# Second model: every projection of a layer's middle in one block, with the state space, step sizes, convolutions, rotation and compression woven in

## The reference, cut to what matters

```
h = rmsnorm(x, attn_norm_w[l])
proj = h @ w_in[l]        # 512 x 1024 by 1024 x 2964
(z, xbc, dt_raw, sc_b, sc_c, sc_h, q, k_c, v_c, k_s, v_s, k_w, v_w, g_nsa) = split(proj)
xbc = silu(causal_dwconv(xbc, conv_w, conv_b))         # 4 taps; gives x, B and C
dt  = softplus(dt_raw + dt_bias)                       # 8 heads
y   = state space: (decay * (C B^T)) (x dt) + x d_skip, then * silu(z), then rmsnorm over 512
y_sc = sc_b * causal_dwconv(sc_c * sc_h, sc_conv_w)    # 3 taps
q, k_c, k_s, k_w are rotated; k_c and v_c are cut into 31 overlapping blocks of 32 tokens,
kc = gelu(blocks(k_c) @ w1) @ w2, vc likewise; gates = sigmoid(g_nsa)
y_nsa = sparse attention over kc/vc, k_s/v_s, k_w/v_w
x = x + concat[y, y_sc, y_nsa] @ w_out;   then a convolved feed-forward
```

## Time and profile before

| | us |
|---|---|
| median of 2 runs (4588.11 to 4590.89) | 4589.5 |
| the profiled execution's own time | 4589.26 |
| its span, first to last instruction | 4587.5 |
| middle of layer 0, first projection matmul to first attention matmul | 282.03 |
| middle of layer 1, the same | 281.80 |

### The profile page before, as it was taken

One profiled execution on the slowest core, in us unless ns is written; L12 is line 12 of the kernel. 1 busy time (PEld: TensorE's weight loads), 2 busy tenths in 40 slices (PEclk: granted clock), 3 DMA queues, 4 the chain that ended last, 5 costly groups with the idle time before them and its releaser, 6 DMA issues. The chain is left out here.

```text
span 4587.5 us, 53132 instructions
## 1 busy us (share of the span) xinstructions
PE 4016.8 (88%) x19582; PEld 3037.8 (66%) x19582; DVE 2268.3 (49%) x3774; ACT 1573.5 (34%) x2671; POOL 299.2 (7%) x292
## 2 busy tenths in 40 slices
PE   4896988998999898878899899886879988678998
PEld 2553566777788795645666688664568877456886
DVE  7777674223653562355532555243455524454552
ACT  2044534112442442245421343233344423333431
POOL 1201010001000000000000100102010010201001
PEclk8997999999999999989999999997899999788999
DMA  6602020111222352000022233220123322012332
GB/s 234 202 8 69 18 96 29 56 61 53 92 96 99 115 165 85 35 17 10 24 69 87 81 98 99 81 75 19 38 64 97 100 98 79 14 33 73 96 98 81
DMA packets 83413, 348.84 MB, mean 76 GB/s; under 512 B 9152, under 2 KB 9536, under 8 KB 79680
## 3 DMA queue, kind: packets, MB, share of 16 engines
q1 hardware_dynamic: 69440, 296.59, 20.0%
q0 software_dynamic: 13824, 50.34, 3.4%
HBM read 344.80 MB, written 2.10 MB: 76 GB/s over the span
## 5 line engine op out<-in xcount | busy, mean ns | idle before, releaser
L556 DVE TENSOR_TENSOR split_low<-weight_ring,split_high 128x1024 fp32r<-128x1024 f32 (+1 forms) x412 | 534.3, 1297 | 818.5 <-ACT split_high L548 818.2
L548 ACT ACTIVATE split_high<-weight_ring 128x1024 fp32r<-128x1024 f32 (+1 forms) x430 | 477.9, 1113 | 969.5 <-PE banks L1197 466.2
L1325 PE MATMUL banks<-normed_high,split_high 128*128 128x512 f32 (+1 forms) x1760 | 652.5, 371 | 79.1 <-DVE normed_low L440 37.9
L1325 PE MATMUL banks<-normed_low,split_high 128*128 128x512 f32 (+1 forms) x1760 | 650.1, 369 | 0.0
L1325 PE MATMUL banks<-normed_high,split_low 128*128 128x512 f32 (+1 forms) x1760 | 649.7, 369 | 0.0
L1325 PEld LDWEIGHTS banks<-normed_high,split_high 128*128 128x128 f32 x1760 | 333.9, 190 | 139.9 <-issue 84.4
L1325 PEld LDWEIGHTS banks<-normed_low,split_high 128*128 128x128 f32 x1760 | 334.1, 190 | 55.4
L1325 PEld LDWEIGHTS banks<-normed_high,split_low 128*128 128x128 f32 x1760 | 333.7, 190 | 55.1
L1197 PE MATMUL banks<-hidden_high,split_high 128*128 128x512 f32 (+1 forms) x880 | 325.0, 369 | 7.2 <-DVE split_low L556 7.2
L1197 PE MATMUL banks<-hidden_low,split_high 128*128 128x512 f32 (+1 forms) x880 | 324.5, 369 | 0.0
L1197 PE MATMUL banks<-hidden_high,split_low 128*128 128x512 f32 (+1 forms) x880 | 324.4, 369 | 0.0
(11 more groups left out here) (235 smaller groups left out, 6550.7 us busy)
## 6 DMA issues: line engine op xcount, KB each, us to landing
weight_ring<-in_up SPq DMA_DIRECT2D x220, 512.0 KB, 3.5
weight_ring<-in_down SPq DMA_DIRECT2D x80, 704.0 KB, 4.0
modulation_ring<-in_ada POOLq DMA_DIRECT2D x96, 512.0 KB, 4.5
weight_ring<-in_merge SPq DMA_DIRECT2D x48, 768.0 KB, 4.2
weight_ring<-in_out SPq DMA_DIRECT2D x32, 512.0 KB, 3.5
weight_ring<-in_diff SPq DMA_DIRECT2D x12, 1024.0 KB, 5.5
weight_ring<-in_xbc SPq DMA_DIRECT2D x16, 512.0 KB, 3.7
weight_ring<-in_window SPq DMA_DIRECT2D x6, 1024.0 KB, 4.8
```

The lines of the kernel that those rows point to most:

```text
L548: act.activation(k.splits[0][:, (n0 + panel) % RING, 0:width], k.slot(n0 + panel)[:, 0:width], ACT.Copy).then_inc(k.high_ready.sem, 1)
L556: dve.tensor_tensor(k.splits[1][:, s, 0:width], k.ring[:, s, 0:width], k.splits[0][:, s, 0:width].bitcast(F32), ALU.subtract).then_inc(k.l ...
L1325: last = pe.matmul(sums(r, half), w, x, start=(c + j == 0), stop=(c == KT - 1 and j == 2))
```

## The change

`project_split`, `short_convolution`, `step_sizes`, `state_space` and `compress` go, and with them the separate norm and rotation blocks. `second_branches` runs one block of 25 jobs, from the norm to the end of the compression. Job 0 is a new full panel that holds dt (columns 0 to 7) and the gates (32 to 43) feature-major, in place of the 20-column token-major jobs. Jobs 1 to 8 are the convolved panels, 9 to 12 the gating panels, 13 to 18 the six short-convolution panels, 19 the compressed keys and values, 20 and 21 the queries, 22 and 23 the other keys, 24 the values. Results rotate through three PSUM banks instead of eight. The steps of the other branches stand between jobs in each engine's queue. The compression's weights no longer pass through the panel ring: SyncE loads them in four DMAs (512 KB each) into the tile of the B-C products once the state space has ended. `branch_tiles` grows from 35 to 40 tiles, and the split ring's slots shrink from 11 to 8 x 128 numbers.

```diff
+    def bank(q):
+        return k.psum[:, q % 3, 0:LAT]
...
+        @block.sync
+        def _(sp):
+            for panel in range(LAST_JOB + 1):
+                sp.wait_ge(*k.low_ready(panel + 1))
+                k.load_panel(sp, n0 + panel + RING)
+                if panel == WITH_HEADS + HEADS:
+                    sp.wait_ge(*k.output_ready(4 * HEADS))
+                    for part in range(4):
+                        sp.dma_start(cmp_weights[:, part, :], k.inp[f"cmp2_{l}"][part]).then_inc(
+                            k.blocks_landed.sem, 16)
...
+            def job(q, between=None):            # PE
+                pe.wait_ge(*k.low_ready(q + 1))
+                if q >= 3:
+                    if 1 <= q - 3 <= CONVOLVED:
+                        pe.wait_ge(*k.taps_added(3 * (q - 3)))
+                    else:
+                        pe.wait_ge(*stored(q - 3))
...
+            job(0)
+            for m in range(CONVOLVED):
+                job(1 + m)
+                if m == 4:
+                    turn_steps()
+            job(9)
+            turn_x()
+            job(10)
+            products_of_group(0)
+            job(11)
+            products_of_group(1)
+            job(12)
+            for h in range(HEADS):
+                spread_total(h)
+                job(WITH_HEADS + h)
+                weigh_head(h)
+            job(21)
+            swap(0)
+            swap(1)
+            job(22)
+            swap(2)
+            multiply_blocks()
+            job(23)
+            swap(3)
+            turn_blocks()
+            sum_squares()
+            job(LAST_JOB, last_swap)
...
+            for m in range(CONVOLVED):           # ScalarE
+                next_high(1 + m)
+                act.wait_ge(*k.product_ready(m + 2))
+                act.activation(targets[1 + m], bank(1 + m), ACT.Identity, bias=..., scale=...)
+                if m == 0: ... act.activation(temporary[1], temporary[0], ACT.Exp, scale=-1.0)
+                elif m == 1: ... act.activation(temporary[2], temporary[0], ACT.Ln)
+                elif m == 5: ... two small copies, then act.activation(gates, ..., ACT.Sigmoid)
+                if m >= 1:
+                    gate(m - 1)                  # Silu
...
+            for h in range(HEADS):
+                next_high(WITH_HEADS + h)
+                for j in range(4):
+                    act.wait_ge(*k.decay_argument(4 * h + j + 1))
+                    act.activation(view, view, ACT.Exp).then_inc(k.decay_ready.sem, 1)
+                store(WITH_HEADS + h, ...)
...
+            next_low(0)                          # VectorE
+            dve.wait_ge(*stored(0))
+            link(dve.tensor_scalar(r1, r0, -1.0, None, ALU.mult))
+            dve.tensor_tensor(r1, r1, r0, ALU.max).then_inc(k.steps_value.sem, 1)
+            next_low(1)
+            taps(0)
+            dve.wait_ge(*k.steps_argument(2))
+            dve.tensor_scalar(r1, r2, 1.0, None, ALU.add).then_inc(k.steps_value.sem, 1)
+            dve.wait_ge(*k.steps_value(2))
             link(dve.tensor_scalar(r3, r1, -1.0, None, ALU.add))
             link(dve.tensor_scalar(r5, r3, 1e-30, None, ALU.max))
             link(dve.reciprocal(r5, r5))
+            next_low(2)
+            taps(1)
+            dve.wait_ge(*k.steps_argument(3))
             link(dve.tensor_tensor(r4, r4, r5, ALU.mult))
             ...                                  # four more on 8 partitions
+            next_low(3)
+            taps(2)
             link(dve.tensor_scalar(r1, r0, k.scalars[0:8, 13:14], -1.0, ALU.mult, ALU.mult))
             link(dve.memset(r2, 1.0))
+            dve.tensor_tensor_scan(r3, r2, r1, 0.0, ALU.mult, ALU.add).then_inc(k.steps_value.sem, 1)
+            for m in range(3, CONVOLVED):
+                next_low(1 + m)
+                taps(m)
...
+            for h in range(HEADS):
+                dve.wait_ge(*k.scores_ready(h + 1))
+                ...                              # the four subtractions of head h
+                next_low(WITH_HEADS + h)
+                if h >= 2 and h % 2 == 0:
+                    finish_pair(h // 2 - 1)
+                if h >= 6:
+                    convolve(h - 6)
+            next_low(21)
+            finish_pair(3)
+            rotate(0)
+            gather()
+            rotate(1)
+            next_low(22)
+            rotate(2)
+            next_low(23)
+            rotate(3)
+            ...                                  # reciprocal, rotate(4), scaling of the 4 tiles
```

More of the change, by code:

```diff
@@ L583, in split_parts @@
     return k.splits[0][:, s, at:at + width], k.splits[1][:, s, at:at + width]
[L586 to L692, removed]
@@ L1617, in _ @@
[L1617 to L1637, removed]
-            link(dve.tensor_scalar(r1, r0, -1.0, None, ALU.mult))
[L1639 to L1643, removed]
+                    link(dve.scalar_tensor_tensor(y[:, shift:LAT], u[:, 0:LAT - shift], weights[:, 2 - shift, m:m + 1],
+                                                  y[:, shift:LAT], ALU.mult, ALU.add))
@@ new lines, in convolve, with rotate @@
+                dve.tensor_tensor(y, y, short[m], ALU.mult)
+            def rotate(r):
+                tile_, rows = turns[r]
+                dve.wait_ge(*k.rope_swapped(r + 1))
+                if r >= 1:
+                    dve.wait_ge(*k.roped(r))
+                dve.tensor_tensor(rope_scratch[0:rows, 2, :], k.psum[0:rows, 7, 0:LAT], k.table("sin_64")[0:rows],
+                                  ALU.mult).then_inc(k.sine_part.sem, 1)
+                dve.wait_ge(*k.cosine_part(r + 1))
+                dve.wait_ge(*k.sine_part(r + 1))
+                dve.tensor_tensor(tile_[0:rows], rope_scratch[0:rows, r % 2, :], rope_scratch[0:rows, 2, :],
+                                  ALU.add).then_inc(k.roped.sem, 1)
@@ new lines, in gather @@
+            def gather():
+                strips = both.rearrange("p (a b) -> p a b", b=16)
+                dve.wait_ge(*k.output_ready(4 * HEADS))
+                dve.memset(gathered, 0.0).then_inc(k.blocks_gathered.sem, 1)
+                dve.wait_ge(*k.blocks_gathered(1))
+                dve.wait_ge(*k.roped(1))
+                for part in range(2):
+                    rows = slice(64 * part, 64 * part + 64)
+                    for half in range(2):
+                        pos = k.vec(f"cmp_pos{l}")[rows, 16 * half:16 * half + 16].unsqueeze(1).to_broadcast(
+                            [64, B, 16])
+                        dve.tensor_tensor(gathered[rows, 32 * part:32 * part + B, 16 * half:16 * half + 16],
+                                          strips[rows, half:half + B, :], pos, ALU.add).then_inc(
+                                              k.blocks_gathered.sem, 1)
@@ L1854, in plain_norm @@
-def plain_norm(k, gain, target, split=None, summed=True, ahead=0, block=None):
-    norm(k, [[(k.stream[:, c, CTX:T], target[:, c, :], lambda s, c=c: gain[:, c:c + 1], None)
-              for c in range(KT)]], D, [(0, LAT, 0)], split,
-         summed=summed, ahead=ahead, block=block)
-def load_constants(k, target, name):
-    with k.nc.Block() as block:
-        @block.sync
-        def _(sp):
-            sp.dma_start(target, k.inp[name]).then_inc(k.constants_loaded.sem, 16)
-    k.ends(constants_loaded=16)
```

566 lines of the change are left out of this document (325 added, 241 removed).

## The result

The changed kernel takes 4442.4 us (two runs, 4439.71 to 4445.15) against 4589.5: a ratio of 0.968, 95% interval 0.9638 to 0.9721. Forecast were 4438.0 in a range of 4414 to 4488. Four more runs of it, on the chip of the first experiments, have a median of 4443.96 against 4588.25 (0.9689, interval 0.9673 to 0.9706).

A forecast was written before the change was run, and what follows sets the result against it. TensorE's one queue was taken to bound the kernel: 196.0 us to issue plus 10.2 of waits make a middle of 206.2, saving 75.8 and 75.6 us in the two layers; 4589.3 less 151.4 gives 4437.9 us, range 4414 to 4488.

The forecast's parts named there:

- The sum: A layer's middle, first projection matmul to first of attention, takes 206.2 us; 151.4 us saved in both layers, 4437.9 in all.
- The floor: What PE must issue in one layer's new block, added up job by job: 196.0 us.
- A round of a head: Spread 0.91, full job 5.44 and weighing 2.27 us on PE: 8.6 us for each of eight heads.
- Turning x and the B-C products: PE work in the middle, busy 7.9 us before the change and taken as 7.9 after it.
- The block products: PE work of the compression: 4 x 2.08 = 8.3 us.
- The waits: PE's waits in a layer's middle: 7.6 us among the first jobs, 1.7 before job 8, 0.9 at swap 1; together 10.2.
- swap 1: Needs the same bank as swap 0 and waits for VectorE's sine product: 0.9 us.
- What was costed at nothing: Short convolution, head chains, rotation and gathering, norm and block-weight transfers lie beside PE's work and add 0 us.
- The covers: PE work hiding other engines' chains; without it the short convolution would cost 7.7 us, a head's chain up to 6.0.
- The head's chain: From a head's spread to GpSimd's fourth product: 6.0 us, 7.0 with contention, hidden because PE needs that piece at 8.4.
- The clock rival: Small f32 products and short waits between jobs could hold PE at half clock; 4668 us with all 24 jobs; chance 0.03.
- Visible hand-offs: Waits between PE and three other engines show between the jobs: 24 us a layer, 4486 us; chance 0.11.

The follow-up runs named there:

- the run with nearly all waits gone: Changed kernel with the steps spread, plus gates' Silus lagging two rounds, sigmoid behind the convolved rounds, odd swaps in bank 5: 4422.91 us, ratio 0.9640.
- the steps spread: Changed kernel with each split of the next panel ahead of the step-size operations, these spread over six rounds, steps turned two jobs later: 4426.24 us, ratio 0.9649.
- the run with four more products: Changed kernel with GpSimd making all four products of each head twice, the extra ones into a tile nothing reads: 4483.12 us, ratio 0.9766.
- All undone together: Changed kernel with heads, tail, step sizes and short convolution each alone, and 96 matmuls of 20 columns before job 12: 4564.15 us, ratio 0.9937.
- the second trace: Changed kernel as it is, run again beside the variants: middles 206.09 and 207.50 us, median 4443.96 us, ratio 0.9689.

## Why the prediction was right, point by point

- **The sum.** Forecast 206.2 us a middle, measured 206.1 and 207.5. The profiled execution took 4439.7 where the sum said 4437.9: +1.2 in the middles, +4.4 and +1.7 in the attention and beyond, -5.5 ahead of the first middle. The last three I had set to nothing; that they nearly cancel is luck. The 1.2 us are all in layer 1, where the half clock behind the one pause lasted twice as long.
- **The floor**, 196.0. In the run with nearly all waits gone PE is busy for 196.2. That it fits so closely is partly luck: terms within it were off and cancel. A round of a head takes 9.01 us, not 8.62: from the spread's start to the job's first matmul are 1.05 us instead of 0.91, the job lasts 5.66 instead of 5.44, weighing 2.30 instead of 2.27. That is 8 x 0.39 = 3.1 us. Turning x and the B-C products I had carried over at the 7.9 us of today, but that row had a mean clock of 0.80; at full clock they took 5.8 (1.66 and twice 2.07). The block products took 7.4 as one row of 64 matmuls instead of 8.3. The other terms are each off by less than 1 us, in both directions, and jobs that follow small products took up to 5.9 us instead of 5.44.
- **The waits**, 10.2. Measured 8.3 in layer 0: 3.64 before job 3 (3.8 forecast), 1.5 for its half clock (2.4), 1.0 before job 5 and 1.3 before job 8 (1.7), 0.9 at swap 1 (0.9). Whether a pause of this length costs the clock was left open, between 5.9 and 7.6 us up to job 5. It does: these jobs lost 6.6 us in layer 0 and 8.1 in layer 1 (from job 2's first matmul to job 5's, less three times 5.44). The runs with the steps spread and all waits taken away show that all but 0.9 us of it was order, not work.
- **What was costed at nothing** stayed at nothing: short convolution, head chains, rotation and gathering, norm, transfers. The covers are real ones: taken away singly they cost 12, 14, 13 us and, for the step sizes, 8.
- **The head's chain** is the one estimate whose margin was thinner than I said: 7.46 us in head 2 (from the spread at 3091.34 to the end of GpSimd's products at 3098.80), where the row had given 6.0 and, with contention, 7.0. Over the heads of layer 0 it was 7.0 to 7.5 us, and 7.9 in heads 6 and 7.

```profile
3091.34 1.12 PE L1621 MATMUL banks<-branch_tiles,tables 8*128 8x512 f32 x2
3092.50 1.93 DVE L1927 TENSOR_SCALAR probs<-banks,branch_tiles 128x512 f32<-128x512 f32 x4 [5.14 <-PE banks L1621]
3094.34 2.03 DVE L565 TENSOR_TENSOR split_low<-weight_ring,split_high 128x1024 fp32r<-128x1024 f32 x1
...
3093.99 4.81 POOL L1801 TENSOR_TENSOR probs<-probs,branch_tiles 128x512 f32<-128x512 f32 x4 [4.65 <-ACT probs L1766]
...
3098.05 2.15 PE L1631 MATMUL banks<-probs,branch_tiles 128*64 128x512 f32 x6
```

VectorE's split takes 2.03 us beside GpSimd instead of 1.22, GpSimd's four products 4.81 instead of 3.31: both lose, and the chain is 1.5 us longer. It changes no sum, because GpSimd's last piece is due at 8.4. The Trainium skill, "SBUF — State Buffer", section "Who interferes with whom", calls the shared ports an exclusive lock. By that rule the prediction had a chain of 7.9 us, which the trace shows in heads 6 and 7 alone, and those two heads late by 1 to 3 us, which they are not: no wait on GpSimd stands in the table.

- **The clock rival** was right that the clock can fall, and wrong on where. Small f32 products between the jobs did not lower it in the heads (1.00 over 69 us without a pause), nor did the waits of 1.0, 1.3 and 0.9 us before job 5, job 8 and swap 1 (1.00 in both stretches). It fell after the pause of 3.6 us, under 20-column matmuls in an unbroken queue, and in two rounds of the run where each head has small waits. The Trainium skill, "TensorE: Matmul & The Clock Gate", section "A second HAM failure mode: psum-queue depth-cycling", expects the swings from cycling through banks with brief idling; three banks in rotation without a wait did not bring them here, while the waits of the run with four more products did (0.95 over its middle).
- **Visible hand-offs**, the rival with 0.11, are out: no head waits. But 1.0 us more on GpSimd is about all that fits.

**Where the gain of 75 us a layer comes from**, then: heads 14, tail with norm and compression 13, short convolution 12, step sizes 8, the gates' small matmuls 18.8 less the full panel's 5.44, so 13; less 4 to 7 that these share. All undone together, less the full panel, that is 55 and 53 us. The other 21 lie outside the five undone parts, and only the lists of waits explain them. None of the five has a fifth of the gain.

## What to carry to other kernels

Where a queue of dense jobs is the floor, take its duration from steady rows and look for each serial chain's slot in the other engines' queues: a chain may be woven in at next to no cost if every instruction that the next job needs is issued ahead of it. The first order that works leaves waits of this kind: a split behind a reciprocal cost 5 to 7 us a layer here, and swapping them was free. And count a pause with its clock: in these traces one of 3.6 us cost 1.5 us more behind it in one layer and 3.0 in the other, and unbroken matmuls of 20 columns cost 17 us where their first ones ran at a rate of 10.7.

## What was not expected of the hardware

- Moving between the plain f32 products and the full jobs costs PE about 0.39 us a round with no wait in the trace, as measured above; no run separates its parts.
- Attention behind layer 0's middle ran at a mean clock of 0.72 instead of 0.80, 78.0 us instead of 73.5, and repeated it in the second trace; behind layer 1's middle it ran at 0.81. The clock of this stretch can so differ with the same code in it and ahead of it; the cause stays open.
- The same pause of 3.64 us at the same place was followed by 7 matmuls at half clock in layer 0 and by 14 in layer 1. The second trace repeats both lengths of the middle.
